# A gather ring of eight pairs, twelve resident tiles and turned first queries in a two-block transformer kernel

## The reference

```python
def peer_ffn(h, w_query, sub_keys, u_tab, v_tab):          # in blocks of 128 tokens
    q = (hb @ w_query).reshape(128, PEER_HEADS, 2, half)   # 8 heads, 2 halves of 128
    s = jnp.einsum("thpd,hpnd->thpn", q, sub_keys)         # 128 keys for each half
    s_top, i_top = lax.top_k(s, PEER_TOPK)                 # 16 of 128, twice
    ...                                                    # 16 best of the 256 sums, softmax gate
    u = jnp.take(u_tab, expert, axis=0)                    # rows of 1024, 16384 experts
    act = gelu(jnp.einsum("thkd,td->thk", u, hb))
    return jnp.einsum("thk,thkd->td", gate * act, jnp.take(v_tab, expert, axis=0))

def conformer_conv(h, w_pw1, b_pw1, w_dw, ...):
    a = h @ w_pw1 + b_pw1                                  # 1024 -> 2048
    a = a[..., :d] * jax.nn.sigmoid(a[..., d:])            # 8 chunks of 128 features
    ...
```

## Time and profile before

| | us |
|---|---|
| median of 3 runs | 2832.6 |
| lowest and highest | 2831.18, 2832.92 |
| the profiled execution, its own time | 2834.92 |
| its span, first to last instruction | 2833.1 |
| mean granted clock of PE over the span | 0.855 |
| gather stage in the span, first gather issued to last pick used | 310 to 1726 |

### The profile page before, as it was taken

The page is one execution under the profiler, slowest core; times in us unless marked ns, Lnnn a source line. Parts: engine busy times, 40 slices in busy tenths (PEclk is TensorE's granted clock), DMA queues, the critical chain, the costliest instruction groups (busy, mean ns, idle before and its releaser), DMA issues. The chain is left out here.

```text
span 2833.1 us, 39427 instructions
## 1 busy us (share of the span) xinstructions
PE 2173.3 (77%) x12874; PEld 1497.9 (53%) x12874; DVE 1968.9 (69%) x4290; ACT 1261.3 (45%) x3045; POOL 667.1 (24%) x599
## 2 busy tenths in 40 slices
PE   7998866444586678766444446999999999999998
PEld 4545733111364546444211104888668878885787
DVE  2885576777687567865667766778657777775777
ACT  3365323332466346642233324446454454563544
POOL 1410344445334333433444450000000000000000
PEclk9999877555797889888655557999999999999999
DMA  9954899999999999999999995665246656552564
GB/s 347 398 213 165 308 419 421 421 421 421 420 407 401 416 417 415 406 419 418 421 421 421 421 421 217 190 186 161 82 135 188 188 158 188 174 165 62 169 187 148
DMA packets 156746, 846.90 MB, mean 299 GB/s; under 512 B 17329, under 2 KB 17457, under 8 KB 90161
## 3 DMA queue, kind: packets, MB, share of 16 engines
q0 software_dynamic: 85392, 579.38, 49.8%
q1 hardware_dynamic: 69584, 253.86, 27.8%
q10 hardware_dynamic: 1616, 11.69, 1.2%
HBM read 843.80 MB, written 1.05 MB: 298 GB/s over the span
## 5 line engine op out<-in xcount | busy, mean ns | idle before, releaser
L2650 DVE SCALAR_TENSOR_TENSOR arena<-arena 128x1024 f32<-128x1024 f32 x308 | 373.5, 1225 | 195.2 <-DMA arena<-experts,arena 191.2
L1936 PE MATMUL ps<-a_both,w_hi 128*128 128x512 f32 x1408 | 503.0, 400 | 5.8 <-DVEq L2405 2.7
L990 POOL DMA_INDIRECT arena<-experts,arena x308 | 366.2, 1189 | 563.2 <-PE ps L1990 420.5
L1990 PE MATMUL ps<-arena 128*32 128x512 f32 x1232 | 237.4, 858 | 337.8 <-ACT arena L1302 327.7
L1063 ACT ACTIVATE w_hi<-weights 128x512 fp32r<-128x512 f32 x528 | 334.2, 634 | 361.3 <-PE ps L1938 267.8
L2386 DVE TENSOR_TENSOR w_lo<-weights,w_hi 128x512 fp32r<-128x512 f32 x528 | 356.6, 690 | 164.8 <-ACT w_hi L1063 153.2
L1938 PE MATMUL ps<-a_both,w_lo 128*128 128x256 f32 x1408 | 395.7, 281 | 0.0
L1296 ACT ACTIVATE arena<-arena 128x1 f32<-128x1 f32 x512 | 102.1, 199 | 576.7 <-DVE arena L2650 328.9
L1990 PE MATMUL ps<-held,arena 128*32 128x512 f32 x816 | 157.2, 855 | 217.0 <-ACT arena L1302 206.7
L2650 DVE SCALAR_TENSOR_TENSOR held<-held,arena 128x1024 f32<-128x1024 f32 x204 | 247.2, 1224 | 109.9 <-DMA held<-experts,arena 107.0
L990 POOL DMA_INDIRECT held<-experts,arena x204 | 248.3, 1217 | 307.4 <-PE ps L1990 258.8
(11 more groups left out here) (291 smaller groups left out, 3677.9 us busy)
## 6 DMA issues: line engine op xcount, KB each, us to landing
weights<-stream SPq DMA_DIRECT2D x445, 512.0 KB
arena<-mod_rows_in POOLq DMA_DIRECT2D x67, 512.0 KB, 8.4
mod_rows<-mod_rows_in POOLq DMA_DIRECT2D x13, 512.0 KB, 7.4
arena<-experts,arena POOLq DMA_INDIRECT x308
held<-ada_in SPq DMA_DIRECT2D x8, 512.0 KB, 11.9
arena<-ada_in SPq DMA_DIRECT2D x8, 512.0 KB, 15.5
held<-kept_in SPq DMA_DIRECT2D x1, 4096.0 KB, 13.1
arena<-kept_in SPq DMA_DIRECT2D x8, 512.0 KB, 7.3
```

The costliest lines, as they stand in the source:

```text
L990: pool.indirect_dma_start(out=pair_of(k), out_offset=None, in_=experts[k // PICKS], in_offset=bass.IndirectOffsetOnAxis(ap=expert[:, at:at ...
L1936: pe.matmul(dst, w_hi[:, o % 2, cut], a_both[:, :, k, :], start=(k == 0), stop=False, skip_group_check=True)
L1990: ins = pe.matmul(ps[first:first + WAVE, v % 2, :], diag[:, one % DIAGS, :], v_of(one, HALF * half, HALF * (half + 1)), start=(k % WAVE_PI ...
L2650: dve.scalar_tensor_tensor(out=u, in0=u, scalar=1.0, in1=h_rows[:, v % 2, :], op0=ALU.mult, op1=ALU.mult, accum_out=act_raw[:, at:at + 1]) ...
```

## The change

Three things are changed together.

**Ring and memory.** `ARENA_PAIRS` goes from 6 to 4, so the ring has eight pairs (four in `arena`, four in `held`). The first gather that waits for `late` is now number 4, not 6. The 4096 columns that come free hold four more resident tiles.

**Resident tiles.** Twelve tiles (queries 0 to 11 of layer 0) instead of seven are loaded at the mark "queries", all behind the attention's last product, and serve both blocks. Queries 12 to 15 are streamed twice. Pointwise chunks 4 to 7 (eight tiles) are loaded once for both blocks, where chunk 7 (two tiles) was. The semaphore `kept_loaded` is now one for two tiles.

**First queries turned round.** For the first wave's first group (tokens 0 to 31, queries 0 to 7) the 32 token columns are the stationary operand and the weights the moving one, four k-chunks side by side in four column groups (`wave_query`, twice 32 matmuls); two copies on ACT bring the sums to SBUF; eight matmuls against a 32-column constant add the four groups and turn the result (`wave_turn`); one copy puts it in place. Only then come scores 0, rows 0 and `late`. Queries 8 to 15 of block 0 now come behind beats 0 to 7, scores 1 at beat 8, the other 96 columns of queries 0 to 7 at beats 8 to 15. `choose` of group 1 moves from beats 4 to 6 to beats 9 to 11, scores 2 from beat 10 to 18 and its choice from 17, 19, 21 to 21, 23, 25, block 1's norm from beat 3 to 9, and block 1's queries start at beat 18, not 16.

```diff
-KEPT = 7
-KEPT_QUERIES = list(range(9, 16))
+KEPT = 12
+KEPT_QUERIES = list(range(KEPT))
+WAVE_TILES = 8
-KEPT_GLU = [7]
+KEPT_GLU = [4, 5, 6, 7]
+GLU_AT = [0, 1, 2, 3, 8, 9, 10, 11]
-LATE_GROUPS = {16: 8}
-LATE_BEAT = 3
-CHOOSE_1 = 4
-ARENA_PAIRS = 6
+LATE_GROUPS = {2: 8, 16: 8}
+LATE_BEAT = 9
+CHOOSE_1 = 9
+ARENA_PAIRS = 4
...
-    for m in range(2 * H):
-        put("query", 0, 0, m, pe=-1, act=-1)
-        if m == 2 * GROUP_HEADS - 1:
-            put("scores", 0, pe=-1, act=-1)
...
-    put("scores", 1, pe=-1, act=-1)
+    for i in range(2):
+        put("wave_query", i, pe=-1, act=-1)
+    put("wave_turn", 0, pe=-1, act=-1)
+    put("scores", 0, pe=-1, act=-1)
+    put("rows", 0, pe=-1, act=-1)
...
+    for m in range(2 * GROUP_HEADS, 2 * H):
+        put("query", 0, 0, m, pe=m - 2 * GROUP_HEADS, act=m - 2 * GROUP_HEADS + 1)
+    put("scores", 1, pe=2 * GROUP_HEADS, act=2 * GROUP_HEADS)
+    for m in range(2 * GROUP_HEADS):
+        put("query", 0, 0, m, pe=2 * GROUP_HEADS + m, act=2 * GROUP_HEADS + m + 1)
...
-        put("query", 0, 1, m, pe=16 + 3 * m, act=17 + 3 * m)
+        put("query", 0, 1, m, pe=18 + 3 * m, act=19 + 3 * m)
...
-            if step == ("query", 0, 0, SLOTS):
-                kept_at = plan.index
...
-                   ("diag", DIAGS * WAVE), ("y", HALF), ("uv", ARENA_PAIRS * 2 * D),
+                   ("diag", DIAGS * WAVE), ("y", HALF), ("uv", ARENA_PAIRS * 2 * D), ("kept", 4 * D),
...
-        kept = lasting[0:2] + [mod_flat[:, D:2 * D], lasting[2]] + \
-            [arena[:, KEPT_AT + D * i:KEPT_AT + D * (i + 1)] for i in range(3)] + [held[:, k, :] for k in range(2)]
+        kept = lasting[0:2] + [mod_flat[:, D:2 * D], mod_flat[:, 0:D], lasting[2]] + \
+            [arena[:, KEPT_AT + D * i:KEPT_AT + D * (i + 1)] for i in range(3)] + \
+            [R["kept"][:, D * i:D * (i + 1)] for i in range(4)] + [held[:, k, :] for k in range(2)]
...
+                def wave_query(i):
+                    pr = pl["wave_query", i]
+                    claim(pr)
+                    for n in range(4):
+                        t = Kept(4 * i + n, 1)
+                        loaded(t)
+                        for k in range(KC):
+                            if i == 0 and n == 0:
+                                pe.wait_ge(a_ready, FEEDS["first"] - KC + k + 1)
+                            rows = slice(WAVE * (k % COL_GROUPS), WAVE * (k % COL_GROUPS + 1))
+                            ins = pe.matmul(bank(pr)[rows, P * n:P * (n + 1)], a_in[:, k, wave_cols], wt(t, k),
+                                            start=(k < COL_GROUPS), stop=(k >= KC - COL_GROUPS), skip_group_check=True)
+                    finish(ins, pr)
+
+                def wave_turn(_):
+                    pr = pl["wave_turn", 0]
+                    claim(pr)
+                    for m in range(WAVE_TILES):
+                        if m % 4 == 0:
+                            wait_taken(pe, pl["wave_query", m // 4])
+                        ins = pe.matmul(bank(pr)[:, WAVE * m:WAVE * (m + 1)], wave_sums[:, P * m:P * (m + 1)],
+                                        const("token"), start=True, stop=True)
+                    finish(ins, pr)
...
-                    wait_taken(pe, pl["query", l, block_of(l, wave), 2 * (first + GROUP_HEADS) - 1])
+                    wait_taken(pe, pl["query", l, block_of(l, wave), 2 * (first + GROUP_HEADS) - 1] if c else pl["wave_turn", 0])
```

More of the change, by code:

```diff
@@ L224, in put @@
             order[engine].setdefault(beat, []).append((what, *which))
-    for m in range(2 * H):
-        put("query", 0, 0, m, pe=-1, act=-1)
-        if m == 2 * GROUP_HEADS - 1:
-            put("scores", 0, pe=-1, act=-1)
-            put("rows", 0, pe=-1, act=-1)
-            for part in range(3):
-                put("choose", 0, part, dve=-1)
-            put("exps", 0, act=-1)
-            for k in range(KC):
-                put("late", k, pe=-1, dve=k // 4)
-    put("scores", 1, pe=-1, act=-1)
+    for i in range(2):
[3 more added lines that the diff above has]
+    put("rows", 0, pe=-1, act=-1)
+    for part in range(3):
+        put("choose", 0, part, dve=-1)
+    put("exps", 0, act=-1)
+    for k in range(KC):
+        put("late", k, pe=-1, dve=k // 4)
+    for m in range(2 * GROUP_HEADS, 2 * H):
[3 more added lines that the diff above has]
+        put("query", 0, 0, m, pe=2 * GROUP_HEADS + m, act=2 * GROUP_HEADS + m + 1)
     for part in range(3):
@@ L424, in make_plan @@
                     plan.marks.append((plan.index, step))
-                tiles = [Kept(2 * KEPT_GLU.index(step[2]) + e, 2) for e in range(2)]
+                tiles = [Kept(GLU_AT[2 * KEPT_GLU.index(step[2]) + e], 2) for e in range(2)]
             else:
@@ L434, in make_plan @@
                 plan.bank_set = [TAP_BANK]
+            elif what == "wave_query":
+                plan.bank_set = [step[1]]
             elif what == "late":
@@ L722, in bass_two_blocks @@
         held_loaded = sem("held_loaded")
-        kept_loaded = [sem(f"kept_loaded{i}") for i in range(KEPT + 2)]
+        kept_loaded = [sem(f"kept_loaded{i}") for i in range((KEPT + 2) // 2)]
         squares_ready = sem("squares_ready")
@@ L2106, in next_sum @@
                     block_sum(pl["next_sum", b], f"next{b}")
-                steps = {"query": query, "scores": scores, "rows": rows, "late": late, "late_norm": late_norm,
+                steps = {"wave_query": wave_query, "wave_turn": wave_turn, "query": query, "scores": scores, "rows": rows, "late": late, "late_norm": late_norm,
                          "fold": fold, "conv_sum": conv_sum, "pw1": pw1, "taps": taps, "mean": mean, "var": var,
```

28 lines of the change are left out of this document (19 added, 9 removed).

## The result

The changed kernel took 2845.91 us (median of 5; 2843.65 to 2852.79), the kernel before 2832.63 in the same rounds (2831.18 to 2835.67): ratio 1.0045, 95% interval 1.0034 to 1.0056, so 13.3 us slower where I had forecast 3.5 us faster; 2845.9 lies above my range of 2816 to 2843. The execution that was profiled is 6.9 us above its kernel's median.

What follows compares the result with a forecast made beforehand. The gather stage was taken as bound by DMA bytes, plus the time until the first gather and holes without pending DMA. Terms -7.5 + 2 - 3 + 5 = -3.5 us took 2832.6 to 2829 us, range 2816 to 2843.

Steps and rivals of the forecast that it cites:

- turned queries: Start of the gather stage: scores and first gather come 7.5 us earlier; -7.5 us (-8 to -2.5).
- first queries between picks: First picks: PE makes the other first queries between them and gather 16 comes slightly late; +2 us (0 to +6).
- fewer streamed tiles: Block 1's queries and the convolution: fewer tiles to load, only partly counted where PE binds; -3 us (-9 to -1).
- eight pairs in place of ten: Gather stage: each gather waits for the pick eight back, losing time at dry places; +5 us (0 to +14).
- behind the last pick: From 1726 to 2833 us: no edit there, so no term in the sum.
- the third rival: PE at the low clock at the turn and among the first picks: +5.5 us, 2838; chance 0.13.
- one full price: Convolution: of two clear dry places at up to 4.9 us each, one is charged, 5 us.
- the second is one long load in which the loss is counted once: Convolution: reason for charging only one of the two clear dry places, 5 us in all.
- second rival: Ring runs dry at each jam of the convolution, 4.9 us each, and at the start: +15.5 us, 2848; chance 0.15.
- equal total work: Argument against repeated ring losses in the convolution: work between jams is the same, so later jams find fewer picks to lose.
- the 5 us of hole: First picks: the old order with eight pairs would leave 5 us without transfers; the new order avoids it.

Runs made afterwards that it cites:

- u8: The changed kernel without its turn: first queries in the old order, queries 4 to 15 resident, ring of eight; 2848.88 us, ratio 1.0045 to the kernel before.
- r8: The kernel before with a ring of eight pairs and nothing else changed; 2853.24 us against 2832.25, ratio 1.0072.
- t8few: The changed kernel, ring of eight, with only eight resident queries and pointwise chunk 7, its saved tiles streamed again; 2858.82 us, ratio 1.0105 to the kernel before.
- r9: The kernel before with a ring of nine pairs and nothing else changed; 2842.10 us against 2832.63, ratio 1.0030.
- r8n: The kernel before with a ring of eight and DVE's share of the norm behind each convolution two beats later; 2857.30 us, ratio 1.0082.
- t10e: The changed kernel with ten pairs, fewer resident tiles, PSUM bank rotation restored and first beats reordered; 2828.83 us, ratio 0.9978 to the kernel before.
- b10n: The kernel before, ring of ten, with DVE's share of the norm behind each convolution two beats later; 2834.26 us, ratio 1.0007.
- the bank runs: PSUM bank rotation behind the gather moved on by three products in the kernel before (2836.98 us), or restored by one in the turned ten-pair kernel (2833.04 us).
- t10: The changed kernel with its ring back at ten pairs, eight resident queries and pointwise chunks 6 and 7; 2837.90 us, ratio 1.0020 to the kernel before.

## Why the prediction was wrong, step by step

| term | forecast | measured in the stage |
|---|---|---|
| turned queries | -7.5 | -7.8 |
| first queries between picks, with fewer streamed tiles | +2 - 3 = -1 | 10.8 + 7.8 - 18.8 = -0.2 (by u8, +4.4 - 4.6) |
| eight pairs in place of ten | +5 | +18.8 (r8) |
| behind the last pick | 0 | +3.1 |
| sum | -3.5 | +13.9 (medians: +13.3) |

The second row is what is left of the stage when r8's price is taken off, which supposes that the ring costs the same in both orders. With u8 between r8 and after it splits: the tiles are 14.2 - 18.8 = -4.6 (u8's stage against r8's, both over before; twelve tiles fewer behind the first gather), the order 10.8 - 14.2 + 7.8 = +4.4, which takes in four tiles more behind it than u8 has.

**The turned queries** were right in mechanism and size, down to the start of scores. PE's low clock, the third rival, didn't come at the turn: its 16 records took 1.97 us (forecast 1.8; at the low level as long for 8). Among the first picks it came once, at 360 to 370 (granted 0.50), and made the hole there longer.

**The other first queries.** I had 0 to +6 and took 2. Pick 159 stands 5.1 us later behind the first gather than before; r8 alone has 4.9 of that, and 1.3 MB less are moved (409 x 428.51 against 417 x 423.38), 3.1 us; so the new order costs some 3 us by this count, 4.4 by u8's: within the range, above the 2. The place was a little off. Gather 16 was issued at 349.33 - 3.99 = 345.3, near the choice's end at 348 that I had; the hole came some 11 us behind that gather, at the late norm, whose move from beat 5 to 11, into the queries, I had costed at nothing.

**The fewer tiles.** The count behind the first gather was right: I had two tiles of block 1's queries and six pointwise ones, 4.2 MB; the trace has 4.2 MB less. In u8 twelve fewer are worth 4.6 us (I had 3 for eight), and that comes by pick 63, from the query tiles. In the convolution they were worth as little as I said or less: after moves 397 x 592.89 = 235.4 MB there and r8 238.9, and they take 592.9 and 592.7 us. Busy time of the stretch that answers the earlier trace rows, and PE's waits in it, after:

```profile
1063.00:1123.00 60.00, 57.03 (x510) 47.58 (x510) 43.92 (x118) 37.68 (x125) 22.93 (x18) 0.91 0.99 399
...
PE ps L2010 <- ACT arena L1314: 3.7, 1, 3.7
```

The 3.9 us of waits for tiles are gone and PE is 95% busy, as forecast, and the queues have room to spare. But t8few against after says that it isn't always so: there 17.4 us of bytes brought 12.9 by the medians and 9.5 in the traced stage. Between these readings, 0.4 us for a tile (u8 against r8, 4.6 for 12) and 0.9 (12.9 for 14) in place of 1.25, the runs don't decide.

**The ring** is the step that failed, by 14 us. "I take one full price", because "the second is one long load in which the loss is counted once". The size of one price was right (4.9 us; 5.0 at pick 15 of r8), and so was the quiet stretch, which loses nothing. But in sum it is paid four times: once at the start, and three times its size in the convolution's picks, in one step of 4.3 us and several smaller ones. My second rival had about that, at 15.5 us slower with four jams in the convolution and 6 us at the start, and I gave it 0.15; of its places the dry stretch at 860 turned out to cost no more with eight pairs than with ten. The argument against it, equal total work, would need DVE, PE and ACT to be the bound all through the convolution. The earlier trace rows showed shares of 0.82 and 0.92 in two stretches of 10 us, and the whole middle stretch of before has 1.01: the queues were the bound between the jams, and the engines' spare time there let the ring fill. r8's steps show that more than one place is then paid for; why one costs 4.3 us and another 1.5 they don't show. The start I had left out: I said that the new order avoids the 5 us of hole with eight pairs; it put 6.4 us of it at 360 to 385.

From the Trainium skill's fixed cost of a DMA (DMA: Bandwidth & Descriptors, "Anatomy of one DMA") I had worked out that eight pairs would be as good as ten. The runs say otherwise: r9 and r8 cost 9.5 and 21.0 us. (The sum was loose too: by the Trainium skill's 2.0 us there, beside 2.49 us for a pick, 1.8 picks would fill the queues, an estimate, and not one and a half.) A pair's place comes free only with its use on PE, as I had written there.

**Behind the last pick** I wrote "What follows the last pick (1726 to 2833 us) has no edit". The edit was there, in the count of products that a rotation hands on. None of my rivals had it.

## What to carry to other kernels

Where transfers are the bound, a ring's depth is paid for at each place where the engines fall behind and not once for the whole stretch. The transfer time of the pairs taken off is at most the price of one place: here 4.9 us, and 18.8 in sum for two pairs, while one pair cost 5.7 to 9.5. Dips of the DMA share in the profile tell where the ring is too short already; the one at 860 was no part of the price, and the places near 765 and 970 didn't show before. The longest wait inside a jam need not be its cause (r8n), so relieve one engine in both depths and compare the prices. Where banks or slots are dealt out by a running count, an instruction added in one phase reorders the waits of all later ones: compare the phases without an edit too, and bring the count back.

## What the runs showed of the hardware

The clock in the mixers varies between kernels whose code there is the same. Busy time by stretch in the first of the second block's two mixers, before:

```profile
2040.00:2050.00 10.00, 7.44 (x27) 3.29 (x26) 6.76 (x26) 4.59 (x14) 0.00 (x0) 1.00 0.03 3
```

and at the same work in t10e:

```profile
2032.00:2042.00 10.00, 8.72 (x19) 3.78 (x19) 6.22 (x23) 4.43 (x13) 0.00 (x0) 0.52 0.00 1
```

Before, the granted clock is 1.00 (2.4 GHz), in t10e 0.52, so most of the stretch at 1.2 GHz, and t10e loses 4 us there that the banks don't explain; r9 and r8n lost 2.6 and 4.0 us at the same place, u8 and b10n nothing. With the 8 us by which attention's end moves, that is as much as the 12 us by which single executions of one kernel lie apart (before: 2829.8 to 2841.9 in 29 runs), and it is why differences below some 5 us are read here from medians of many runs or from picks counted from a common row. Also, in the bank runs, 2.60 us of waiting on PE in place of 1.87 came with matmuls at 2.07 and 2.08 us for the pair behind it, not 1.13; the granted clock there is 0.50 in t10 and was 1.00 at before's pair. The 0.7 us of longer wait so came with 3.7 us in all at that place.
